# A fifth of eight K pairs by seven products instead of eight in the first feed-forward's gate and up projection

## What is computed

```python
def swiglu(h, w_gate, w_up, w_down):
    return (jax.nn.silu(h @ w_gate) * (h @ w_up)) @ w_down
```

## Time and profile before

| | |
|---|---|
| median of 3 runs | 2572.56 us (2571.4 to 2573.23) |
| the profiled execution, its device time | 2573.23 us |
| the profiled execution, span of its instructions | 2571.4 us |
| TensorE busy | 2561.0 us (100% of the span), 14027 matmuls recorded |
| VectorE busy | 2017.4 us (78%) |
| ScalarE busy | 1507.8 us (59%) |
| GpSimd busy | 328.7 us (13%) |
| DMA | 493.67 MB, 192 GB/s in the mean |

### The profile page before, as it was taken

One profiled execution on the slowest core, in us unless ns is written; L12 is line 12 of the kernel. 1 busy time (PEld: TensorE's weight loads), 2 busy tenths in 40 slices (PEclk: granted clock), 3 DMA queues, 4 the chain that ended last, 5 costly groups with the idle time before them and its releaser, 6 DMA issues.

```text
span 2571.4 us, 36476 instructions
## 1 busy us (share of the span) xinstructions
PE 2561.0 (100%) x14027; PEld 2207.6 (86%) x14027; DVE 2017.4 (78%) x2927; ACT 1507.8 (59%) x2221; POOL 328.7 (13%) x292
## 2 busy tenths in 40 slices
PE   9999999999999999999999999999999999999998
PEld 8888888888889888888888888888888888888887
DVE  7787777777977878899888998887876767666675
ACT  6666658776656555555555566445654545455554
POOL 2111103316201001111111152101100000000000
PEclk9999999999999999999999999999999999999999
DMA  7565666565656556666566556556566666665664
GB/s 246 182 221 182 191 201 197 174 204 196 206 176 199 169 180 197 197 196 197 195 196 194 194 180 222 155 172 197 188 197 190 190 193 189 193 191 190 191 191 159
DMA packets 137351, 493.67 MB, mean 192 GB/s; under 512 B 15447, under 2 KB 16344, under 8 KB 136792
## 3 DMA queue, kind: packets, MB, share of 16 engines
q1 hardware_dynamic: 136600, 490.80, 60.5%
q10 hardware_dynamic: 576, 0.53, 0.1%
HBM read 489.14 MB, written 2.13 MB: 191 GB/s over the span
## 4 chain that ended last, share of the span: by engine, by line
PE 98%; DVE 1%; ACT 1%; issue 0%; DMA 0%; ACTq 0%
PE ps L1180 46%; PE ps L1177 23%; PE ps L1096 5%; PE ps L1098 5%; PE ps L1097 5%; PE ps L1150 4%; PE ps L1152 4%; PE ps L1151 4%; PE ps L1194 1%; DVE wl L1835 1%; PE ps L1320 0%; PE ps L1165 0%; PE ps L1166 0%; PE ps L1167 0%; ACT wh L1437 0%; ACT T L1437 0%
## 5 line engine op out<-in xcount | busy, mean ns | idle before, releaser
L1835 DVE TENSOR_TENSOR wl<-raw,wh 128x1024 fp32r<-128x1024 f32 (+2 forms) x908 | 1119.6, 1241 | 389.0 <-ACT wh L1437 388.0
L1437 ACT ACTIVATE wh<-raw 128x1024 fp32r<-128x1024 f32 (+2 forms) x908 | 938.5, 1039 | 635.9 <-PE ps L1177 391.6
L1180 PE MATMUL ps<-X,wh 128*128 128x512 f32 x3600 | 1204.9, 395 | 0.8 <-DVE X L1841 0.8
L1177 PE MATMUL ps<-X,wl 128*128 128x256 f32 x3600 | 904.3, 278 | 0.0
L1180 PEld LDWEIGHTS ps<-X,wh 128*128 128x128 f32 x3600 | 652.3, 188 | 127.9 <-issue 2.3
L1177 PEld LDWEIGHTS ps<-X,wl 128*128 128x128 f32 x3600 | 660.7, 188 | 31.2
L1180 PE MATMUL ps<-XG,wh 128*128 128x512 f32 x1472 | 491.6, 395 | 1.3 <-DVE hT L1835 1.3
L1177 PE MATMUL ps<-XG,wl 128*128 128x256 f32 x1472 | 366.8, 278 | 0.0
L1180 PEld LDWEIGHTS ps<-XG,wh 128*128 128x128 f32 x1472 | 265.3, 188 | 51.9 <-DVE hT L1835 1.6
L1177 PEld LDWEIGHTS ps<-XG,wl 128*128 128x128 f32 x1472 | 269.7, 188 | 14.2
L1437 ACT ACTIVATE T<-ps 128x256 f32<-128x256 f32 (+1 forms) x380 | 126.6, 383 | 192.9 <-PE ps L1177 192.2
(11 more groups left out here) (257 smaller groups left out, 2467.9 us busy)
## 6 DMA issues: line engine op xcount, KB each, us to landing
raw<-in_w_down SPq DMA_DIRECT2D x176, 512.0 KB, 3.6
raw<-in_w_gu SPq DMA_DIRECT2D x144, 512.0 KB, 3.7
raw<-in_w_gate SPq DMA_DIRECT2D x104, 512.0 KB, 3.5
raw<-in_w_sc SPq DMA_DIRECT2D x95, 512.0 KB, 4.0
raw<-in_w_val SPq DMA_DIRECT2D x88, 512.0 KB, 3.5
raw<-in_w_zx SPq DMA_DIRECT2D x80, 512.0 KB, 3.6
raw<-in_w_in SPq DMA_DIRECT2D x56, 512.0 KB, 3.6
raw<-in_w_osc SPq DMA_DIRECT2D x32, 512.0 KB, 3.7
```

The lines of the kernel that those rows point to most:

```text
L1177: t = e.matmul(bank(c, i)[:, 0:256], wl[:, b0:b0 + 128], X[:, kx * 512:kx * 512 + 256], start=False, stop=sp and kk == c.kn - 1)
L1180: e.matmul(bank(c, i)[:, :], wh[:, b0:b0 + 128], X[:, kx * 512:kx * 512 + 512], start=st and kk == 0, stop=False)
L1437: return e.activation(out, in_, ACT.Copy, scale=scale)
L1835: return e.tensor_tensor(out, a, b, op)
```

## The change

The pattern of groups 4 to 10 becomes SCSSCSSC: five pairs summed, three plain, and two summed pairs stand directly behind each other in two places. Group 3 becomes CCSSCSSC, with four summed. Both lists of sums and of plain pairs are numbered in order, so the K tiles go with the pattern. `NS` becomes 5, the fifth `Sx` takes the words where `Tc` lay, `Tc` and `Td` move up by 1024 words, and the pieces `sb0` to `sb2` begin two steps earlier, so that they end at the step where they ended before.

```diff
-PATTERN = {2: "CCCCCCCC", 3: "CCSCSCSC"}
+PATTERN = {2: "CCCCCCCC", 3: "CCSSCSSC"}
 NG = 9
-NS = 4
+NS = 5
...
         col = add("G", q, "w_gu", q - 2, (), "1", ph, w=512, pair=4, run=False)
-        pattern = PATTERN.get(q, "SCSCSCSC")
+        pattern = PATTERN.get(q, "SCSSCSSC")
...
     for j in range(NS):
-        s = GROUPS[0].first + 7 + 2 * j
+        s = GROUPS[0].first + 5 + 2 * j
...
-    Tc, Td = a_(7680, 1024), a_(8704, 1024)
+    Tc, Td = a_(8704, 1024), a_(9728, 1024)
```

## The result

| | before | changed kernel |
|---|---|---|
| median | 2572.57 us (2571.4 to 2573.23, 4 runs) | 2591.07 us (2590.94 to 2593.26, 4 runs) |
| profiled execution, device time | 2573.23 us | 2593.26 us |
| its span | 2571.4 us | 2591.4 us |
| matmuls recorded | 14027 | 14003 |

By the means of the runs the changed kernel takes 1.0074 times as long, with a 95% interval of 1.0057 to 1.0092; by the medians it takes 18.5 us more.

What follows compares the result with a forecast made beforehand. TensorE was taken to set the end, with VectorE 90% busy in one period. 2573.23 less 4.7 saved plus 20.3 of waits gave 2588.8, or 2588.2 against the median; 8 in 10 from 2580 to 2597.

Steps and rivals of the forecast that it cites:

- What is removed: On TensorE, each of eight pairs turned from plain to summed saves 0.59 us, 4.7 us in all.
- The wait at two summed pairs in a row: TensorE waits 1.27 us for VectorE before unit c of the second pair, in 16 places, 20.3 us.
- Nothing is handed on: Behind the late unit c nothing more is late, so each of 16 places pays its own 1.27 us.
- the signs that it had named for wrong steps: Second pair's split of b well before t = 2.7, waits at other units, or no waits and a time near 2568.
- Edits costed at nothing: Fifth token-side sum in group 2, covered by VectorE's idle time (else about 1.7 us once), moved buffers and unchanged loads: 0.
- The sum: Whole kernel: 2573.23 - 4.7 + 20.3 = 2588.8, or 2588.2 against the median, 0.6% slower.
- The late tiles: Rival, chance 0.12: tiles behind two neighbouring summed pairs outrun 0.55 us of slack, 0.8 us a group, 6.4 in all, 2594.6.
- The edges of a group: At group ends, VectorE's 0.4 us less lead is absorbed, 0; rival, chance 0.08: 3 us over seven groups, 2591.
- The other side: Rival, chance 0.05: VectorE's lead covers two summed pairs, mean load 15.24 of 15.20 us, so only the saving counts: 2567.9.

Runs made afterwards that it cites:

- the last run: Changed kernel with a fifth place for wh and wl in groups 3 to 10 and only half of each w_gu tile loaded: 2574.25 us, ratio 1.0007.

## Why the prediction was right

**What is removed** held. 0.59 us a pair by starts; the run with one pair fewer gave 0.56, and the busy durations were indeed no measure.

**The wait at two summed pairs in a row** held to 0.01 us: 1.28 against 1.27, with the two splits at t = 2.74 and 6.95 (2.74 and 6.94 worked out), in 16 places. That it comes from the order was then shown from four sides: neighbours without added work bring it, cutting `tc` shortens it by `tc`'s length, moving `tc` shortens it without any change of work, and a plain unit put in the way inherits it.

**Nothing is handed on** held for the first neighbours of each group and for the second in five of eight groups; in three the second wait was longer, by 0.31, 0.03 and 0.08 us. Of the signs that it had named for wrong steps one did appear, ScalarE waiting for the DMA in every group, and with it one small wait at another unit (0.22).

**Edits costed at nothing** held: the run with these alone is at 0.9998.

**The sum** was 2.9 us short (18.5 measured, 15.6 worked out). Two terms were missing. Behind each of the 16 waits the second matmul starts 0.10 us later than usual, 1.6 us. The late tiles, which the prediction had as a rival with a chance of 0.12 for all of 6.4 us, came in as part: each of the tiles was late, but the 0.55 us of slack covered it save in three groups, and halving them gave back 0.5 us. With these the sum is 17.7 of the medians' 18.5. The profiled execution can be added up in full. Its span is 20.0 us above the one before: 16 x 1.38 = 22.1 for the waits and what follows them, less 4.7, then 0.4 for the three lengthened waits, 0.8 for the transposes, and 1.7 at the very start, ahead of the change, where one and the same product on GpSimd (R<-T,A) began at 49.01 before and at 50.72 after. That makes 20.3. The medians do not show the part at the start. Small slips in the working carry nothing: 12.49 + 4.20 + 1.22 is 17.91 and not 18.00, and `td` was over at t = 7.03 where 7.07 stands.

**The edges of a group**, put at nothing with 3 us as the other end, were small but not nothing. The old seven waits are as long as before. The 0.8 us at the transposes lie there, behind two groups in place of all. In the run with half loads that line is back at 0.4 us in one wait, which points to the loads and not to VectorE's shorter lead; it was not tested by itself.

**The other side** (as counted, 2567.9) fell. Its argument, a mean load of 15.24 against 15.20 us, was true as a mean: the last run, with the ring and the late w_gu tiles out of the way, came to 2574.25. No run brought the change below the kernel before; the fastest with five pairs summed and nothing left out is the one with the fifth place, at 2582.96. A fifth place in `raw` was not tried, since only 1024 words of A were left and `tc` reads two places that lie side by side.

## What to carry to other kernels

Where one engine prepares operands for another through a short ring, its mean load says little: take the point at which the ring lets the next preparation begin, add up what stands in the preparing engine's own list from there to the operand, and set that against the consumer's time over the same units. A cheaper algorithm on the consumer (seven products for eight, 0.59 us saved) that loads the preparing engine (4.2 us more) is worth it only where idle time stands inside that stretch, and putting two such pieces side by side costs more (1.38 us) than either saves. Before deepening the ring, look for what is late next; here a tile 1.5 us late was harmless behind the old wait and cost 8.7 us once that was shortened.

## What the runs showed of the hardware

- A matmul of 128x512 that follows a wait is followed by the next after 0.33 us, not 0.23 (1061.15 to 1061.48). In the changed kernel's profile it was 0.33 or 0.34 at all 23 waits of 0.49 us and more, and 0.29 at the one of 0.22.
- The wait that the weight-loading side shows (1.55 us) is 0.27 us longer than the gap that the matmul starts show (1.28), and the matmul side's (1.11) is 0.17 shorter. Only the starts gave the cost.
- Half the bytes did not land in half the time: over the stretch from 1043 to 1078 us a w_gu tile of 512 KB took 4.2 us from issue to landing in the median (the changed kernel), one of 256 KB 2.6 (the run with half loads).
